# DeltaNet in a hybrid decoder layer: unnormalised queries, z in token order, first-level masks multiplied in beforehand, jobs in a new order

## The chip, the cores and the metric

The kernel runs on one core of one Trainium2 chip. The metric is the device time of one execution in microseconds (us); less is better. Five engines work side by side, each through its own instruction queue in program order: TensorE (PE, with its weight loads shown as PEld), VectorE (DVE), ScalarE (ACT), GpSimd (POOL) and SyncE (SP, which here starts the DMAs). They wait for one another by semaphores only.

## What is computed

One decoder layer over 256 tokens of width 2048: RMSNorm, one wide projection, two mixers side by side (a gated DeltaNet and a sliding-window attention), a gated merge, an output projection, and an MLP. All of it is in float32; each big matrix product is done as three fast ones, with the weights and the activations split into a high and a low part. The change touches the DeltaNet alone. Cut to what matters:

```python
qkv_c = silu(causal_depthwise_conv(qkv, conv_w))          # 4 taps along the tokens
q, k, v = split(qkv_c, 3)                                 # 16 heads of 128
q = q * rsqrt(sum(q * q) + 1e-6)                          # l2_normalize, per token and head
k = k * rsqrt(sum(k * k) + 1e-6)
beta = sigmoid(b_logit);  g = -exp(a_log) * softplus(a_logit + dt_bias)
q = q * 128 ** -0.5                                       # chunks of 64 tokens from here
gamma = exp(where(causal, decay_i - decay_j, -inf))       # decay = cumsum(g)
a_low = where(strict, (k * beta) @ k.T * gamma, 0)
sol   = solve(a_low + eye(64), [v * beta, k * beta * exp(decay)])
qk    = (q @ k.T) * gamma
# for each of the 4 chunks in turn, with the state S (128 x 128 per head):
v_new = u - w @ S
o     = (q * exp(decay)) @ S + qk @ v_new
S     = S * chunk_decay + k_dec.T @ v_new
o = rms_norm(o, norm_g) * silu(z)
```

## The kernel before

**Big products.** PE takes 512 output columns at a time (an *output*, `output`, lines 269 to 293). One output has 8 chunks of weights; each chunk is a DMA of 512 KB into `raw`, which ACT copies to `w_hi` (`split`, L653) and DVE turns into `w_lo` (L996). Chunk c+3 is split at the head of the work for chunk c on both engines. A chunk gives PE two *steps* of six matmuls each (L287 to L289).

**DeltaNet jobs.** Four windows of four outputs (k, q, v and z of four heads) feed `rawg`. While PE runs the 64 steps of one window, the DeltaNet of the four heads before (a *group*) is done in between: after step h of the big product every engine calls `gdn_step(h, g)`, which holds the job that belongs to this step. The steps stand in a table by hand (L66 to L74). Each of PE, ACT and DVE walks the same list in its own queue: for chunk c first `split(c + 3)`, then the jobs of step 2c, then those of step 2c+1; after the last chunk of an output it reads the accumulator (`read`, L875 and L1284). A job that must wait for another engine holds up all that stands behind it in its queue. GpSimd has a list of its own (`group`, L1415 to L1452). The group g = 3 runs in five straight outputs behind the loop.

**The steps of a group**, with their number in the table before:
- `FRONT` (k 0, q 1, v 25, z 37): PE turns the projected tile by 8 transposes (L316), ACT takes it with the fourth tap of the convolution (L726; for z it takes the tanh, L711).
- `TAPS`, `TANH`, `SILU`: DVE adds the other taps (L1051, three jobs each), ACT makes the tanh of half of it (L732), DVE makes the silu (L1057).
- `BACK` (k 10, q 16, v 34): PE turns it back (L345). For k and q ACT squares and sums 8 tiles (L738), DVE scales the sums (L1039), GpSimd raises them to the power -1/2 (`power`, L1418), and ACT multiplies (`NORM`, k 13, q 19, L744).
- `TK` 16 and `TQ` 21: PE turns the normalised k and q again (L354), ACT and DVE copy them to `kq` (L750, L755, L1076).
- `ROWS` 11: PE adds up the decays (L361, L362), DVE and ACT make the exponentials (L1068 to L1071, L759 to L761), GpSimd multiplies masks in (L1427 to L1434).
- `KKQ` 22: PE multiplies k by k and q by k (L376); DVE multiplies the results with the masked gammas (L1081 to L1083). GpSimd (L1437 to L1440) and DVE (L1087, L1089) make the matrices of the first level of the inverse from them.
- `INV` 25: five levels of a blockwise inverse, each with a first pass at step 25+3l and a second at 26+3l (L384); ACT copies in between (L765), DVE subtracts (L1093, L1096).
- `QTM` 40, then `P1`, `P2`, `P3`: the recurrence over four chunks (L423, L432, L440; ACT L775; DVE L1112, L1119, L1127).
- the end: the sum of squares of o (ACT L781), its power -1/2, o times it (DVE L1136), `OT` 63: PE turns o (L316), DVE multiplies with gain and silu(z) (L1145), ACT and DVE split it into `og_hi` and `og_lo`.

Of the kernel before, what the change touches and what calls it, by code (L numbers as in the profile page):

```python
# [1553 lines left out]
```

## Time and profile before

| | |
|---|---|
| median of 3 runs | 1945.68 us (1942.75 to 1945.89) |
| the profiled execution | 1942.99 us, of it 1941.2 us span |
| PE busy | 1885.3 us, 97% of the span |
| DVE / ACT / POOL busy | 1099.7 / 885.4 / 120.6 us |
| granted TensorE clock, mean | 0.989 |

The profile shows one execution. A line of the groups names the source line, the engine, the operation and its tile, then the count, the busy time and the mean of one, then how long the engine stood idle just before and what ended that. "PEclk" is the share of full speed that TensorE was granted. The four groups of the DeltaNet lie between about 121 and 740 us.

### The profile page before, as it was taken

The page shows a single profiled execution, that of the slowest core. Times are in us where ns is not written, and L with a number is a line of the kernel's source. Part 1 is how long each engine was busy: PE and PEld are TensorE (multiplying, and loading weights), DVE is VectorE, ACT ScalarE, POOL GpSimd, SP SyncE. Part 2 cuts the span into 40 slices and gives each one's busy share as a digit, 9 for nine tenths or more (in the row PEclk, how much of TensorE's full clock was granted, in tenths as well). Part 3 has the DMA queues.
Part 4 walks back from the last instruction along what each step waited for, and adds up shares of the span by engine and source line. Part 5 has one row for each costly group of instructions (what it writes and reads, how often), then busy time and mean ns, then how long its engine had stood idle before and what let it go on. Part 6 is the DMA issues. An engine that isn't in the chain of part 4 may idle for free.

```text
span 1941.2 us, 29129 instructions
## 1 busy us (share of the span) xinstructions
PE 1885.3 (97%) x10816; PEld 1554.7 (80%) x10816; DVE 1099.7 (57%) x1438; ACT 885.4 (46%) x1382; POOL 120.6 (6%) x86
## 2 busy tenths in 40 slices
PE   7998998998998999999999999999999999999997
PEld 6887877877877888888888888888888888888886
DVE  5366676676676665666555555555544455555544
ACT  5344345354354345555444445444433344444442
POOL 0005014014014000000000000000000000000000
PEclk9899999999999999999999999999999999999999
DMA  7353333333333354444456666555555555555553
GB/s 256 126 163 119 110 131 109 110 130 109 115 124 115 114 167 152 141 152 141 161 195 201 201 199 208 183 189 177 191 192 192 192 190 189 185 186 192 195 191 124
DMA packets 87953, 316.36 MB, mean 163 GB/s; under 512 B 9648, under 2 KB 10160, under 8 KB 87728
## 3 DMA queue, kind: packets, MB, share of 16 engines
q1 hardware_dynamic: 86992, 312.64, 48.9%
q0 software_dynamic: 576, 2.10, 0.4%
q8 instruction: 78, 1.28, 0.3%
q10 hardware_dynamic: 288, 0.18, 0.0%
q14 instruction: 19, 0.16, 0.0%
HBM read 312.79 MB, written 2.10 MB: 162 GB/s over the span
## 4 chain that ended last, share of the span: by engine, by line
PE 53%; issue 38%; DVE 3%; POOL 3%; ACT 1%; DMA 0%; DVEq 0%; ACTq 0%; POOLq 0%; SPq 0%
PE acc L287 15%; PE acc L289 14%; PE acc L288 14%; PE J L384 4%; PE J L432 1%; PE J L316 1%; POOL rg L1418 1%; PE J L423 1%; ACT w_hi L653 1%; PE J L440 1%; DVE cT L1051 1%; DVE qn L1051 1%; PE J L475 1%; PE J L304 0%; POOL mats L1440 0%
## 5 line engine op out<-in xcount | busy, mean ns | idle before, releaser
L996 DVE TENSOR_TENSOR w_lo<-raw,w_hi 128x1024 fp32r<-128x1024 f32 x584 | 725.3, 1244 | 638.0 <-ACT w_hi L653 636.6
L653 ACT ACTIVATE w_hi<-raw 128x1024 fp32r<-128x1024 f32 x584 | 618.7, 1061 | 681.7 <-PE acc L289 679.0
L287 PE MATMUL acc<-w_hi,hT_hi 128*128 128x512 f32 x1440 | 582.1, 404 | 8.9 <-issue 4.4
L289 PE MATMUL acc<-w_hi,hT_lo 128*128 128x512 f32 x1440 | 564.7, 392 | 0.0
L288 PE MATMUL acc<-w_lo,hT_hi 128*128 128x512 f32 x1440 | 564.5, 392 | 0.0
L287 PEld LDWEIGHTS acc<-w_hi,hT_hi 128*128 128x128 f32 x1440 | 272.4, 189 | 71.8 <-issue 8.4
L289 PEld LDWEIGHTS acc<-w_hi,hT_lo 128*128 128x128 f32 x1440 | 272.1, 189 | 58.7
L288 PEld LDWEIGHTS acc<-w_lo,hT_hi 128*128 128x128 f32 x1440 | 272.6, 189 | 52.5 <-issue 1.0
L287 PE MATMUL acc<-w_hi,act_hi 128*128 128x512 f32 x512 | 199.3, 389 | 0.0
L289 PE MATMUL acc<-w_hi,act_lo 128*128 128x512 f32 x512 | 199.2, 389 | 0.0
L288 PE MATMUL acc<-w_lo,act_hi 128*128 128x512 f32 x512 | 199.2, 389 | 0.0
L289 PEld LDWEIGHTS acc<-w_hi,act_lo 128*128 128x128 f32 x512 | 96.1, 188 | 20.1
L287 PEld LDWEIGHTS acc<-w_hi,act_hi 128*128 128x128 f32 x512 | 96.1, 188 | 19.9
L288 PEld LDWEIGHTS acc<-w_lo,act_hi 128*128 128x128 f32 x512 | 96.1, 188 | 19.7
L287 PE MATMUL acc<-w_hi,og_hi 128*128 128x512 f32 x256 | 102.2, 399 | 0.0
L289 PE MATMUL acc<-w_hi,og_lo 128*128 128x512 f32 x256 | 99.8, 390 | 0.0
L288 PE MATMUL acc<-w_lo,og_hi 128*128 128x512 f32 x256 | 99.8, 390 | 0.0
L384 PEld LDWEIGHTS J<-mats 64*64 64x64 f32 x2048 | 66.5, 140 | 24.9 <-issue 24.9
L384 PE MATMUL J<-mats 64*64 64x64 f32 x2048 | 72.6, 226 | 10.7 <-POOL mats L1440 10.7
L287 PEld LDWEIGHTS acc<-w_hi,og_hi 128*128 128x128 f32 x256 | 48.1, 188 | 11.9 <-issue 2.7
L289 PEld LDWEIGHTS acc<-w_hi,og_lo 128*128 128x128 f32 x256 | 48.1, 188 | 10.4
L288 PEld LDWEIGHTS acc<-w_lo,og_hi 128*128 128x128 f32 x256 | 48.1, 188 | 9.2
(210 smaller groups left out, 1522.4 us busy)
## 6 DMA issues: line engine op xcount, KB each, us to landing
raw<-weights SPq DMA_DIRECT2D x584, 512.0 KB, 3.3
xres<-x SPq DMA_DIRECT2D x4, 512.0 KB, 7.5
xres<-x POOLq DMA_DIRECT2D x4, 512.0 KB, 5.6
y<-nat SPq DMA_DIRECT2D x4, 512.0 KB, 2.7
fgain_sb<-fgain SPq DMA_DIRECT2D x1, 1024.0 KB, 5.2
masks_sb<-masks SPq DMA_DIRECT2D x1, 640.0 KB, 11.0
zs<-w_ba SPq DMA_DIRECT2D x1, 256.0 KB, 9.9
dist_sb<-dist SPq DMA_DIRECT2D x1, 192.0 KB, 3.4
```

The source lines that it names most:

```text
L287: mm(o, aT_hi[:, kt, tok], w_hi[:, c % RING, w], start=(c == 0 and k == 0), stop=False)
L288: mm(o, aT_hi[:, kt, tok], w_lo[:, c % RING, w], start=False, stop=False)
L289: last = mm(o, aT_lo[:, kt, tok], w_hi[:, c % RING, w], start=False, stop=(c == nch - 1 and k == CK - 1))
L316: ins = tr(J[:, b0 + m // 2, (m % 2) * T + t * P:(m % 2) * T + (t + 1) * P], src[:, t, m * P:(m + 1) * P], ident)
L384: ins = mm(J[r, bank, u * C:(u + 1) * C], lhs[r, u], rhs[r, u], start=True, stop=True)
L423: ins = mm(J[:, 0, hd * P:(hd + 1) * P], kq[:, hd, c * P:(c + 1) * P], S[:, hd], start=True, stop=True)
L432: ins = mm(J[:, 1, hd * P:(hd + 1) * P], solve[kr, t * HG + hd].rearrange("p a c -> p (a c)"), RH[kr, hd * P:(hd + 1) * P], start=True, st ...
L440: ins = mm(J[:, 2, hd * P:(hd + 1) * P], kn[kr, t, hd * P:(hd + 1) * P], VO[kr, hd * P:(hd + 1) * P], start=True, stop=True)
L475: ins = tr(J[:, 2 + pb, b * P:(b + 1) * P], prob[:, pb, b * P:(b + 1) * P], ident)
L653: A(w_hi[:, slot], raw[:, slot], ACT.Copy).then_inc(hi_ready, 1)
L996: tt(w_lo[:, slot], raw[:, slot], w_hi[:, slot].bitcast(F32), ALU.subtract).then_inc(lo_ready, 1)
L1051: ins = stt(out=dst[:, m, s:T], in0=J[:, b, o:o + T - s], scalar=cwg[:, n, m, 3 - s:4 - s], in1=dst[:, m, s:T], op0=ALU.mult, op1=ALU.add)
```

## The change

It does four things.
- **Queries.** q is no longer normalised ahead of the products. Its silu is written straight into `kq` in token order on the free axis; BACK q only serves the sum of squares, `NORM` q, `TQ` and the copies behind it are gone. Since rms_norm follows, the length of q enters as a larger epsilon (`rg[:, 3]`, `nq_done`) in the scale of o.
- **z.** It stays in token order: no turn at `FRONT`, one tanh of 1024 columns and one product (`Z_TANH` 34 and 35). The halves of 64 tokens are swapped when the accumulator is read (`halves`), so that each reading of z is two instructions instead of one. The product of o with its scale now takes silu(z) with it: eight instructions on DVE in place of one. Behind `OT`, ACT makes `og_hi` from PSUM by four instructions, and DVE `og_lo` by four.
- **Masks.** GpSimd multiplies `nlow1` and `nup1` into the gammas ahead of `KKQ`; behind it DVE has four products and two additions of the identity, GpSimd only the masks of the levels.
- **Order.** A new table: `ROWS` at 2, `FRONT` q at 7, `BACK` k at 9, `NORM_K` 11, `TK` 14, `KKQ` 17, `BACK` q 19, `INV` 22, `QTM` 37, `OT` 62.

```diff
-FRONT = {ITEM_K: 0, ITEM_Q: 1, ITEM_V: 25, ITEM_Z: 37}
-BANK = {ITEM_K: 0, ITEM_Q: 2, ITEM_V: 2, ITEM_Z: 2}
-TAPS = {ITEM_K: (0, 1, 2), ITEM_Q: (3, 5, 7), ITEM_V: (26, 28, 31)}
-TANH = {ITEM_K: 3, ITEM_Q: 9, ITEM_V: 32}
-SILU = {ITEM_K: 4, ITEM_Q: 10, ITEM_V: 33}
-BACK = {ITEM_K: 10, ITEM_Q: 16, ITEM_V: 34}
-NORM = {ITEM_K: 13, ITEM_Q: 19}
-ROWS, TK, TQ, KKQ, INV, QTM, OT = 11, 16, 21, 22, 25, 40, 63
-P1, P2, P3 = (40, 45, 50, 55), (42, 47, 52, 57), (44, 49, 54, None)
+FRONT = {ITEM_K: 0, ITEM_Q: 7, ITEM_V: 25}
+BANK = {ITEM_K: 0, ITEM_Q: 2, ITEM_V: 2}
+TAPS = {ITEM_K: (0, 1, 3), ITEM_Q: (9, 11, 12), ITEM_V: (26, 28, 30)}
+TANH = {ITEM_K: 4, ITEM_Q: 13, ITEM_V: 31}
+SILU = {ITEM_K: 5, ITEM_Q: 15, ITEM_V: 32}
+BACK = {ITEM_K: 9, ITEM_Q: 19, ITEM_V: 34}
+ROWS, ROWS_EXP, NORM_K, TK, KKQ, INV, Z_TANH, QTM, OT = 2, 3, 11, 14, 17, 22, 34, 37, 62
+P1, P2, P3 = (37, 42, 47, 52), (39, 44, 49, 55), (41, 46, 51, None)
+O_SQ, O_SUM, O_SCALE = (48, 56), 57, 60
 
 PAIRS = HQ // 2
...
                 if h == KKQ:
 
-                    pe.wait_ge(kq_a, 2 * g + 2)
+                    pe.wait_ge(kq_a, g + 1)
                     pe.wait_ge(kq_d, g + 1)
 
+                    pe.wait_ge(silu_done, 4 * g + 2)
                     pe.sem_inc(step_begun, 1)
...
+                for n in (ITEM_K, ITEM_Q, ITEM_V):
+                    if h == BACK[n]:
+                        pe.wait_ge(silu_done, 4 * g + (n + 1))
+                        if n == ITEM_Q:
+
+                            pe.wait_ge(xu_link, g + 1)
+                        for t in range(NT):
+                            for m in range(HG):
+                                src = kq_q(m, t) if n == ITEM_Q else cT[:, m, t * P:(t + 1) * P]
+                                ins = tr(J[:, BANK[n] + t, m * P:(m + 1) * P], src, ident)
+                        ins.then_inc(back_T, 1)
+                if h == TK:
+
+                    pe.wait_ge(norm_done, g + 1)
+                    for t in range(NT):
+                        for m in range(HG):
+                            ins = tr(J[:, t, m * P:(m + 1) * P], kn[:, t, m * P:(m + 1) * P], ident)
+                    ins.then_inc(qk_T, 1)
 
...
-                    if h == NORM[n]:
-                        act.wait_ge(nr_done, 2 * g + (n + 1))
-                        for u in range(U):
-                            ins = A(dst3[:, u], J[:, BANK[n] + u // HG, (u % HG) * P:(u % HG + 1) * P], ACT.Copy,
-                                    scale=rg[:, n, u:u + 1])
-                        ins.then_inc(norm_done, 1)
+                if h == NORM_K:
+                    act.wait_ge(nr_done, g + 1)
+                    for u in range(U):
+                        ins = A(kn3[:, u], J[:, u // HG, (u % HG) * P:(u % HG + 1) * P], ACT.Copy, scale=rg[:, 0, u:u + 1])
+                    ins.then_inc(norm_done, 1)
                 if h == TK:
-                    act.wait_ge(qk_T, 2 * g + 1)
+                    act.wait_ge(qk_T, g + 1)
                     dst = kq[:, :, 0:T].rearrange("p h (a c) -> p h a c", a=4)[:, :, 0:4:3]
                     A(dst, J[:, 0].rearrange("p (h a c) -> p h a c", h=HG, a=2), ACT.Copy).then_inc(kq_a, 1)
-                if h == TQ:
-
-                    act.wait_ge(qk_T, 2 * g + 2)
-                    for t in range(NT):
-                        ins = A(kq[:, :, t * T + C:t * T + C + P], J[:, 2 + t].rearrange("p (h t) -> p h t", h=HG), ACT.Copy)
-                    ins.then_inc(kq_a, 1)
-                if h == ROWS:
+                if h == Z_TANH:
+
+                    act.wait_ge(silu_done, 4 * g + 3)
+                    act.wait_ge(rawg_a, 4 * g + 4)
+                    act.wait_ge(rawg_d, 4 * g + 4)
+                    A(zs2, z_raw, ACT.Tanh, scale=0.5).then_inc(tanh_done, 1)
+                if h == ROWS_EXP:
                     act.wait_ge(arg_done, g + 1)
                     A(mat(M_X), mat(M_X), ACT.Exp)
...
                 if h == OT:
+                    act.wait_ge(o_T, g + 1)
                     for b in range(2):
-                        act.wait_ge(og_f, 2 * g + (3 + b))
-                        A(og_hi[:, bass.ds(g * HG + 2 * b, 2), :], cT[:, 2 * b:2 * b + 2], ACT.Copy).then_inc(og_hi_done, 1)
+                        src = J[:, b].rearrange("p (u a c) -> p u a c", u=4, a=2)
+                        dst = og_hi[:, bass.ds(g * HG + 2 * b, 2), :].rearrange("p h (t a c) -> p (h t) a c", t=NT, a=2)
+                        for a in range(2):
+                            ins = A(dst[:, :, a], src[:, :, 1 - a], ACT.Copy, scale=gdn_gain)
+                        ins.then_inc(og_hi_done, 1)
 
...
+                        if n == ITEM_Z:
+                            for r, to in halves():
+                                ins = A(rawg[to, n, 0], acc[r, n % 2, 0], ACT.Copy, scale=row_scale(0, 0)[r])
+                            ins.then_inc(rawg_a, 1)
+                        else:
+                            A(rawg[:, n, 0], acc[:, n % 2, 0], ACT.Copy, scale=row_scale(0, 0)).then_inc(rawg_a, 1)
...
+                if h == BACK[ITEM_Q] + 1:
+                    dve.wait_ge(nsq_done, 2 * g + 2)
+
+
+                    f = 4 * EPS * P
+                    for r, to in halves():
+                        ins = ts(rg[to, 3], rg[r, 1], f, 4 * EPS * f, ALU.mult, ALU.add)
+                    ins.then_inc(nq_done, 1)
...
-                        dst, th = (qnT, vbT) if n == ITEM_Q else (cT[:], zs[:])
-                        stt(out=dst, in0=th, scalar=1.0, in1=dst, op0=ALU.add, op1=ALU.mult).then_inc(silu_done, 1)
+                        if n == ITEM_Q:
+                            dst = kq[:].rearrange("p h (t e) -> p h t e", t=NT)[:, :, :, C:C + P]
+                            src, th = (a.rearrange("p h (t e) -> p h t e", t=NT) for a in (qnT, vbT))
+                        else:
+                            dst, src, th = cT[:], cT[:], zs[:]
+                        stt(out=dst, in0=th, scalar=1.0, in1=src, op0=ALU.add, op1=ALU.mult).then_inc(silu_done, 1)
...
                     dve.wait_ge(kkq_done, g + 1)
-                    dve.wait_ge(mask_done, 5 * g + 5)
+                    dve.wait_ge(mask_done, 6 * g + 6)
                     kk, kqp = (J[:, b].rearrange("p (u c) -> p u c", u=U) for b in (2, 3))
-                    tt(mat(M_V), kk, mat(M_V), ALU.mult)
-                    tt(mat(M_AT), kk, mat(M_B1), ALU.mult)
-                    tt(mat(M_KQ), kqp, mat(M_KQ), ALU.mult).then_inc(at_ready, 1)
+                    tt(mat(M_AT), kk, mat(M_B1), ALU.mult).then_inc(at_ready, 1)
+                    tt(mat(M_X), kk, mat(M_V), ALU.mult)
+                    tt(mat(M_U), kk, mat(M_U), ALU.mult)
+                    tt(mat(M_KQ), kqp, mat(M_KQ), ALU.mult).then_inc(xu_link, 1)
                 if h == KKQ + 1:
 
-                    dve.wait_ge(at_ready, g + 1)
-                    tt(mat(M_U), mat(M_AT), over(nup1, U), ALU.mult).then_inc(u0_ready, 1)
-                    dve.wait_ge(u0_ready, 2 * g + 1)
+                    dve.wait_ge(xu_link, g + 1)
+                    tt(mat(M_X), mat(M_X), over(eye64, U), ALU.add)
                     tt(mat(M_U), mat(M_U), over(eye64, U), ALU.add).then_inc(u0_ready, 1)
                 for lv in range(LEVELS):
                     if h == INV + 3 * lv + 1:
...
+                    dve.wait_ge(nq_done, g + 1)
+                    stt(out=rg[:, 2], in0=rg[:, 2], scalar=4.0 / P, in1=rg[:, 3], op0=ALU.mult, op1=ALU.add).then_inc(ossq_done, 1)
+                if h == O_SCALE:
                     dve.wait_ge(or_done, g + 1)
-                    tt(qn3, qn3, wide(rg[:, 2], P), ALU.mult).then_inc(on_done, 1)
+                    dve.wait_ge(silu_done, 4 * g + 4)
+                    for u in range(U):
+                        ins = stt(out=qn3[:, u], in0=qn3[:, u], scalar=rg[:, 2, u:u + 1], in1=zs3[:, u], op0=ALU.mult, op1=ALU.mult)
+                    ins.then_inc(on_done, 1)
                 if h == OT:
...
-                power(0, nssq_done, 2 * g + 1, nr_done)
 
                 pool.wait_ge(exp_done, g + 1)
                 tt(mat(M_KQ), mat(M_X), over(upi, U), ALU.mult).then_inc(mask_done, 1)
                 tt(mat(M_B1), mat(M_X), mat(M_B0), ALU.mult).then_inc(mask_done, 1)
-                pool.wait_ge(mask_done, 5 * g + 2)
+                power(0, nssq_done, g + 1, nr_done)
+                pool.wait_ge(mask_done, 6 * g + 2)
                 tt(mat(M_B1), mat(M_B1), over(up, U), ALU.mult).then_inc(mask_done, 1)
-                tt(mat(M_V), mat(M_U), over(low, U), ALU.mult).then_inc(mask_done, 1)
-                power(1, nssq_done, 2 * g + 2, nr_done)
-                pool.wait_ge(mask_done, 5 * g + 4)
+                tt(mat(M_V), mat(M_U), over(nlow1, U), ALU.mult).then_inc(mask_done, 1)
+                pool.wait_ge(mask_done, 6 * g + 4)
                 tt(mat(M_V), mat(M_V), wide(scu(BETA), C), ALU.mult).then_inc(mask_done, 1)
+                tt(mat(M_U), mat(M_B1), over(nup1, U), ALU.mult).then_inc(mask_done, 1)
 
                 pool.wait_ge(at_ready, g + 1)
-                tt(mat(M_X), mat(M_V), over(nlow1, U), ALU.mult).then_inc(xu_link, 1)
                 tt(mat(M_B0), mat(M_AT), over(up_level[0], U), ALU.mult).then_inc(bt_ready, 1)
-                pool.wait_ge(xu_link, g + 1)
-                tt(mat(M_X), mat(M_X), over(eye64, U), ALU.add).then_inc(x0_ready, 1)
                 for lv in range(1, LEVELS):
                     if lv >= 2:
 
@@ -1445,7 +1457,7 @@
                     tt(mat(M_B0 + lv % 2), mat(M_AT), over(up_level[lv], U), ALU.mult).then_inc(bt_ready, 1)
                     if lv == 1:
 
-                        pool.wait_ge(qk_T, 2 * g + 1)
+                        pool.wait_ge(qk_T, g + 1)
                         tt(kn3, kn3, wide(scu(K_DEC), P), ALU.mult).then_inc(kdec_done, 1)
```

## Rows read from the trace of the kernel before

**Rows 1.** The page: two of its costliest groups, busy us and mean ns.

```profile
L996 DVE TENSOR_TENSOR w_lo<-raw,w_hi 128x1024 fp32r<-128x1024 f32 x584 | 725.3, 1244 | 638.0 <-ACT w_hi L653 636.6
L653 ACT ACTIVATE w_hi<-raw 128x1024 fp32r<-128x1024 f32 x584 | 618.7, 1061 | 681.7 <-PE acc L289 679.0
```

**Rows 2.** Waits of PE: who waited for whom, us in total, times, longest.

```profile
PE J L354 <- ACT qn L744: 10.9, 4, 3.0
PE J L384 <- POOL mats L1440: 10.7, 4, 2.7
...
PE J L354 <- ACT kn L744: 3.5, 4, 0.9
PE J L361 <- DVE qn L1051: 3.1, 3, 1.6
```

**Rows 3.** Timeline of PE, group 1: start us, us, engine, line, what.

```profile
266.06 1.03 PE L316 MATMUL J<-masks_sb,rawg 128*128 128x128 f32 x8
...
268.31 1.03 PE L316 MATMUL J<-masks_sb,rawg 128*128 128x128 f32 x8
...
297.64 0.39 PE L287 MATMUL acc<-w_hi,hT_hi 128*128 128x512 f32 x1
...
299.00 0.39 PE L287 MATMUL acc<-w_hi,hT_hi 128*128 128x512 f32 x1
```

**Rows 4.** Timeline of PE at the inverse, groups 1 and 2 (the latter from 462).

```profile
318.66 1.97 PE L384 MATMUL J<-mats 64*64 64x64 f32 x32 [2.68 <-POOL mats L1440]
...
324.71 0.50 PE L287 MATMUL acc<-w_hi,hT_hi 128*128 128x512 f32 x1
...
327.66 1.15 PE L384 MATMUL J<-mats 64*64 64x64 f32 x32
...
332.35 0.50 PE L287 MATMUL acc<-w_hi,hT_hi 128*128 128x512 f32 x1
...
462.18 1.97 PE L384 MATMUL J<-mats 64*64 64x64 f32 x32 [2.69 <-POOL mats L1440]
...
469.67 0.49 PE L287 MATMUL acc<-w_hi,hT_hi 128*128 128x512 f32 x1
```

**Rows 5.** Busy us by stretches: PE, PEld, DVE, ACT, POOL, then PEclk, DMA share.

```profile
320.00:323.00 3.00, 3.00 (x28) 2.25 (x27) 0.75 (x1) 1.54 (x2) 2.89 (x2) 0.70 0.10 37
```

**Rows 6.** Timeline of ACT, group 1.

```profile
284.72 1.06 ACT L732 ACTIVATE vb<-qn 128x1024 f32<-128x1024 f32 x1 [4.78 <-DVE qn L1051]
...
286.63 0.26 ACT L738 ACTIVATE kn<-J 128x128 f32<-128x128 f32 x1
...
288.54 0.25 ACT L738 ACTIVATION_READ_ACCUMULATOR kn<-J 128x1 f32 x1
...
293.11 2.16 ACT L744 ACTIVATE kn<-J,rg 128x128 f32<-128x128 f32 x8
```

**Rows 7.** Timeline of DVE, group 1.

```profile
283.05 1.64 DVE L1051 SCALAR_TENSOR_TENSOR qn<-J,cwg,qn 128x253 f32<-128x253 f32 x4
...
287.90 1.22 DVE L1057 SCALAR_TENSOR_TENSOR qn<-vb,qn 128x1024 f32<-128x1024 f32 x1
289.03 0.17 DVE L1039 TENSOR_SCALAR rg<-rg 128x8 f32<-128x8 f32 x1
...
296.25 2.05 DVE L996 TENSOR_TENSOR w_lo<-raw,w_hi 128x1024 fp32r<-128x1024 f32 x1 [1.54 <-ACT w_hi L653]
...
300.45 0.68 DVE L1076 COPY kq<-J 128x512 f32<-128x512 f32 x1
...
390.78 1.13 DVE L1127 SCALAR_TENSOR_TENSOR S<-S,scg,J 128x128 f32<-128x128 f32 x4
```

**Rows 8.** Timeline of POOL, group 1.

```profile
269.35 1.04 POOL L1423 TENSOR_TENSOR mats<-scg,masks_sb 128x512 f32<-128x512 f32 x1
289.28 1.64 POOL L1418 TENSOR_TENSOR rg<-rg,stat 128x8 f32<-128x8 f32 x1 [18.88 <-DVE rg L1039]
...
301.29 2.71 POOL L1418 TENSOR_TENSOR rg<-rg,stat 128x8 f32<-128x8 f32 x1 [1.84 <-DVE rg L1039]
```

More of the change, by code:

```diff
@@ L169, in hybrid_trunk, with kq_q, halves @@
         qnT, vbT = (a[:].rearrange("p t n -> p (t n)").rearrange("p (h t) -> p h t", h=HG) for a in (qn, vb))
+        zs2 = zs[:].rearrange("p h t -> p (h t)")
+        zs3 = zs2.rearrange("p (u e) -> p u e", u=U)
+        z_raw = rawg[:, ITEM_Z].rearrange("p t n -> p (t n)")
+        def kq_q(m, t):
+            return kq[:, m, t * T + C:t * T + C + P]
+        def halves():
+            return [(slice(ck * C, ck * C + C), slice((1 - ck) * C, (2 - ck) * C)) for ck in range(2)]
         qn3, kn3, vb3 = (a[:].rearrange("p t (h e) -> p (t h) e", h=HG) for a in (qn, kn, vb))
@@ L705, in gdn_step @@
             def gdn_step(h, g):
-                if h == FRONT[ITEM_Z]:
-                    act.wait_ge(front_T, 4 * g + 4)
-                    act.wait_ge(silu_done, 4 * g + 3)
-                    for b in range(2):
-                        ins = A(zs[:, 2 * b:2 * b + 2].rearrange("p a t -> p (a t)"), J[:, 2 + b], ACT.Tanh, scale=0.5)
-                    ins.then_inc(tanh_done, 1)
                 for n in (ITEM_K, ITEM_Q, ITEM_V):
                     if h == FRONT[n]:
-                        act.wait_ge(front_T, 4 * g + (n + 1))
+                        act.wait_ge(front_T, 3 * g + (n + 1))
                         if n == ITEM_K:
                             act.wait_ge(par_ready, g + 1)
-                        else:
-                            if n == ITEM_V:
-                                act.wait_ge(back_T, 3 * g + 2)
+                        if n == ITEM_V:
+                            act.wait_ge(back_T, 3 * g + 2)
                         dst = qnT if n == ITEM_Q else cT
@@ L914, in gate @@
                 return ops
-            act.wait_ge(og_lo_done, 2 * NG)
+            act.wait_ge(og_lo_done, 2 * NG + 2)
             def mix1(j):
@@ L1026, in gdn_step @@
                     V.tensor_copy(cwg[:], conv_w[:, :, bass.ds(g * HG, HG), :]).then_inc(par_ready, 1)
-                if h == FRONT[ITEM_Z] + 1:
+                if h == Z_TANH + 1:
                     dve.wait_ge(tanh_done, 4 * g + 4)
-                    for b in range(2):
-                        zb = zs[:, 2 * b:2 * b + 2].rearrange("p a t -> p (a t)")
-                        ins = stt(out=zb, in0=zb, scalar=1.0, in1=J[:, 2 + b], op0=ALU.add, op1=ALU.mult)
-                    ins.then_inc(silu_done, 1)
-                for i, n, dst in ((0, ITEM_K, kn3), (1, ITEM_Q, qn3)):
-                    if h == BACK[n] + 1:
-                        dve.wait_ge(nsq_done, 2 * g + (i + 1))
-                        f = (1.0, float(P))[i]
-                        ts(rg[:, i], rg[:, i], f, 4 * EPS * f, ALU.mult, ALU.add).then_inc(nssq_done, 1)
+                    stt(out=zs2, in0=zs2, scalar=1.0, in1=z_raw, op0=ALU.add, op1=ALU.mult).then_inc(silu_done, 1)
+                if h == BACK[ITEM_K] + 1:
+                    dve.wait_ge(nsq_done, 2 * g + 1)
+                    ts(rg[:, 0], rg[:, 0], 1.0, 4 * EPS, ALU.mult, ALU.add).then_inc(nssq_done, 1)
+                if h == BACK[ITEM_Q] + 1:
[4 more added lines that the diff above has]
+                    ins.then_inc(nq_done, 1)
                 for n in (ITEM_K, ITEM_Q, ITEM_V):
```

93 lines of the change are left out of this document (36 added, 57 removed).

## The prediction

> **What bounds the kernel now.** I read the page first. TensorE is busy over nearly the whole span, so the time is the sum of what PE issues plus the little it waits. The two groups that take most of DVE and ACT are the splits of the weights, one each per chunk, 1.24 and 1.06 us in the mean [rows 1]; the reader should keep them in mind, because each stands in the same queue as the DeltaNet's jobs. Second I read the waits of PE, which are few and all inside the DeltaNet: before the turn of the normalised q 10.9 us, before the first level of the inverse 10.7 us, before the turn of the normalised k 3.5 us, before ROWS 3.1 us [rows 2]. Together 28.2 us in four groups, 7.05 us a group. Third, the timeline of PE, for what a step costs. Six matmuls of the big product, an ordinary step, take 299.00 - 297.64 = 1.36 us; a step with a turn of eight transposes takes 268.31 - 266.06 = 2.25 us, so a turn costs 0.89 us [rows 3]. Fourth, the timeline at the inverse. After the wait at its first level the two passes and the step between take 324.71 - 318.66 = 6.05 us, and at the next level, undisturbed, 332.35 - 327.66 = 4.69 us [rows 4]. The difference of 1.36 us is the clock: PE was granted 0.70 of full speed in that stretch, thus partly the level of 1.2 GHz instead of 2.4 [rows 5], after two waits within some 16 us. In group 2 the same passes take 469.67 - 462.18 = 7.49 us, a loss of 2.80 [rows 4]. These are the least and the largest of four; I take 1.8 us a group, since three of the four lie near the low end.
>
> So a group now loses 7.05 us to waits and about 1.8 to the clock, 8.85 us.
>
> **The change, part by part.**
>
> *Two turns less.* The turn of z at FRONT and the one at TQ go. Each is 0.89 us of PE time with nothing beside it, for PE is the bound: 1.78 us a group, 7.1 in all.
>
> *The wait at TQ* goes with its job: 10.9 / 4 = 2.7 us a group. *The wait at ROWS* goes too, if GpSimd's tables are there at step 2. Today they end at 269.35 + 1.04 = 270.39 [rows 8], 4.3 us after the window's first turn started at 266.06 [rows 3]. They wait for DVE, which is then still at work on the group before; OT comes a step earlier, 1.36 us, so about 2.9. PE gets to ROWS a turn and two steps after that start, 0.89 + 2.72 = 3.6. The margin is 0.7 us; without the earlier OT the wait would be 0.7.
>
> *The wait at the first level* goes. Today GpSimd makes three products in a row between KKQ and INV, and that is the wait of 2.7 us. After the change GpSimd has one, and DVE makes X and U: four products of the 0.68 us kind (128x512, one operand in PSUM) [rows 7], then a split and two additions. PE has five steps and one turn between KKQ and INV, some 7.8 us; DVE needs 2.8 for the products, up to 2.05 for a split beside GpSimd [rows 7] and at most 1.7 for each addition, about 7.6 with the latencies. It just fits. 2.7 us gone, and if PE has not waited before, 1.8 of the clock with it.
>
> *What becomes late instead.* This is the heart of my forecast. The new table puts only five steps between BACK k (9) and TK (14), with no other PE job in them, and KKQ at 17. I follow the chain from the end of BACK k's transposes on (time 0), with every queue in its order.
> - ACT: squares of k, 288.79 - 286.63 = 2.16 us [rows 6]; then it splits a chunk, about 1.0 once the overlap with the neighbour is taken off its 1.06. 3.15.
> - DVE can't scale the sums before it has split the same chunk (1.24) [rows 1], then 0.17 [rows 7]. 4.5.
> - GpSimd: the power -1/2, 1.64 us [rows 8]. 6.25, with 0.1 for latencies.
> - ACT: NORM_K, 2.16 us [rows 6]. 8.45. TK can start.
> - PE is there after five steps, 5 x 1.36, at 6.65. It waits **1.8 us**, takes the turn (0.89) and three more steps (4.1) and stands at KKQ at 13.45.
> - KKQ also waits for the silu of q (`silu_done`), and that hangs on the same ACT queue: behind NORM_K stands a split (1.0), then DVE's split of that chunk, 1.24 or, beside GpSimd's masks, 2.05 [rows 7]; I take 1.6, between them, as the masks end within it. Then the last tap of q, 1.64 [rows 7]. ACT: the tanh, 1.06 [rows 6], and a split, 1.0. DVE: its split, 1.2, the copy to kq, 0.6, the silu, 1.22 [rows 7]. Sum 8.45 + 1.0 + 1.6 + 1.6 + 1.06 + 1.0 + 1.2 + 0.6 + 1.2 = 17.7.
> - So PE waits another 17.7 - 13.45 = **4.3 us** at KKQ. Both together 6.1 us a group. The whole of this replaces 0.9 + 2.7 + 0.8 us that PE waits ahead of KKQ today.
>
> The power's row is not sure. The one that I take, 1.64 us, ran beside a DVE product with an operand in PSUM; another ran beside DVE's split and took 2.71 [rows 8]. In the new order DVE has a tap of the convolution with an operand in PSUM at that time, so I take 1.64 and keep 1.07 us a group, 4.3 in all, for the range. The Trainium skill (GPSIMD Engine Reference, section 1, Specifications) says that GpSimd shares its SBUF interface with VectorE and meets contention from DVE instructions with two SBUF inputs or in a two-port mode. By that rule the price is the lower one as well; the two rows agree with it.
>
> *The tail.* The scale of o stands at step 60 for OT at 62. DVE's job starts when ACT and DVE have split the chunk of that step, 1.06 + 1.24 and latencies, about 2.4 us after the end of step 59. It is now eight instructions of 128x128; four such take 1.13 [rows 7], eight 2.2. That makes 4.6 or 4.7, and PE is there after three steps, 4.08. A wait of **0.6 us** a group. Below nothing it can't go; above, 1.2, if each instruction costs twice the part that I read from the four.
>
> *The rest.* Four instructions of ACT from PSUM at OT instead of two, DVE's eight products for o, the two halves of z: all beside PE, and the next window's first turn comes over 3 us after OT. Inside the inverse I find one place where ACT's tanh of v stands ahead of the copy for level 3 and comes 0.15 us late; others pass with 0.2 to 0.3 us to spare. 0.15 a group, up to 0.6 when the spare fails. The first BACK q waits for DVE's products, level with PE. No DMA is moved; SP's queue gets nothing new, and the splits run two chunks ahead of PE through all the waits above.
>
> *The clock.* A wait of 4.3 us behind one of 1.8 is longer than any that the trace shows, so I expect PE to fall to 1.2 GHz at KKQ in each group. I price it as the drops of today, 1.8 us; bounds 0 and 2.8 [rows 4].
>
> **The sum.** Today a group loses 7.05 + 1.8 = 8.85, and the clock in group 3 falls once more, about 1.5 in all: 4 x 8.85 + 1.5 = 36.9; with the turns, 7.1, there are 44.0 us to be had. The new group loses 6.1 + 0.6 + 0.15 + 1.8 = 8.65, in four 34.6. The gain is 9.4 us. The profiled execution took 1942.99 us, 1.79 more than its span; it lies 2.7 below the median of the runs. So 1933.6 against that execution, and against the median 1945.68 - 9.4 = **1936.3 us**.
>
> **The rivals.**
> - *The waits really vanish* (the order works as a schedule without stalls). Then only the tail and the inverse cost, 4 x 0.75 = 3: 44.0 - 3 = 41 gained, 1904.7. For it speaks that all four waits of today lose their cause; against it, the chain above, in which every link is a row and the queues are strict. Chance 0.08.
> - *The waits stay but the clock holds.* Gain 9.4 + 7.2, 1929.1. For it speaks that the wait at TQ of 3.0 us, alone, was followed by steps at full speed in group 1. Chance 0.12.
> - *The chain grows and the waits only move.* If the chain from BACK k to the silu of q is 1.4 to 3.3 us longer than I make it, the result is within 0.2% of before; 2.35 us more gives 1945.7. Chance 0.13.
> - *Slower.* GpSimd and DVE get in each other's way in that chain: the power takes 2.71 instead of 1.64, and DVE's two later splits 2.05 instead of 1.6 and 1.2, together 2.4 us a group; with the clock loss at 2.8 instead of 1.8 a group costs 3.4 more than I say, 13.6 in all, which ends at 1949.9. It decides from 2.35 us a group on. Against it: GpSimd's four masks end about when the first of the two splits does. Chance 0.08.
>
> **How the numbers follow.** The forecast itself has 0.59, its own range 1930 to 1942. About 0.2%, 3.9 us, is what a measurement of this kernel can tell from no change. Faster: 0.08 + 0.12 + nearly all of 0.59 = 0.76; same: 0.13 and a little of the forecast, 0.16; slower 0.08. The range leaves out the first rival and most of the last: 1925 to 1945.
>
> **What would show it.** The waits of PE should list TK on ACT's kn with about 1.8 us, four times, and KKQ on DVE's silu of q (L1057 before) with about 4.3, four times, and nothing before the inverse. The page should have 64 transposes less. PE's clock should dip at KKQ and not at the first level. OT should wait 0.6 us for DVE's product of o. I am wrong if PE reaches KKQ without a wait (then ACT's and DVE's queues run ahead of the steps more than I think), or if waits appear in the levels of the inverse, where my margins are thinnest.

## The result, and the profile after

The changed kernel takes **1933.86 us** (median of four runs, 1933.71 to 1933.97), the kernel before beside it 1945.79 (1942.75 to 1948.06). The ratio is 0.994, with a 95% interval of 0.9922 to 0.9957: 0.4 to 0.8% faster. The forecast was 1936.3, range 1925 to 1945.

The page after, its head and its clock:

```profile
span 1932.1 us, 28995 instructions
## 1 busy us (share of the span) xinstructions
PE 1878.6 (97%) x10752; PEld 1549.1 (80%) x10752; DVE 1102.7 (57%) x1466; ACT 877.4 (45%) x1350; POOL 104.2 (5%) x78
...
PEclk9899999999999999999999999999999999999999
```

PE has 64 instructions less, as two turns of eight in four groups must give. The waits of PE in the whole execution (who waited for whom, us in total, times, longest), the answer to [rows 2]:

```profile
PE J L364 <- DVE kq L1067: 15.8, 4, 4.0
PE J L383 <- ACT kn L740: 6.7, 4, 1.7
...
PE J L348 <- POOL mats L1438: 2.4, 2, 1.2
PE J L326 <- DVE qn L1149: 1.8, 4, 0.5
PE acc L297 <- ACT rawg L876: 1.8, 1, 1.8
PE acc L297 <- issue: 1.7, 1, 1.7
```

Three waits of before are gone: that of TQ on ACT, that of the first level of the inverse on GpSimd, and that of ROWS on DVE; ROWS now waits for GpSimd's tables in two of four groups. The first line is new: KKQ (L364) waits for the silu of q (L1067), four times, 4.0 us at the longest. The second is TK, 1.7 where it was 0.9. OT (L326) waits 0.5 us in each group for DVE's eight products of o. The last two lines are the gaps of PE at the start of the two looped windows.

The timeline of PE in group 1 shows the two, and the clock behind the second:

```profile
293.58 1.09 PE L383 MATMUL J<-masks_sb,kn 128*128 128x128 f32 x8 [1.67 <-ACT kn L740]
...
302.70 2.96 PE L364 MATMUL J<-kq 128*64 128x64 f32 x64 [3.92 <-DVE kq L1067]
...
309.11 1.03 PE L376 MATMUL J<-masks_sb,kq 128*128 128x128 f32 x8
...
314.17 1.15 PE L390 MATMUL J<-mats 64*64 64x64 f32 x32
```

From KKQ to the turn of q behind it 309.11 - 302.70 = 6.41 us pass; without the drop it is 4.87 (below). The granted clock of that stretch (columns as in [rows 5]):

```profile
302.00:307.00 5.00, 4.30 (x67) 3.97 (x68) 3.55 (x5) 0.52 (x1) 0.43 (x1) 0.66 0.57 199
```

The first level of the inverse starts at 314.17 without a wait and takes 1.15 us instead of 1.97 [rows 4].

**Where the time went.** The two profiled executions differ by 9.1 us of span, and not all of it is the DeltaNet's. From the first turn of group 0 to the first turn of probabilities in the attention the kernel before takes 734.7 - 122.71 = 612.0 us, the changed one 725.6 - 125.49 = 600.1; from there to the end both take 1206.5 (1941.2 - 734.7, 1932.1 - 725.6). So the DeltaNet gained 11.9 us, and the changed one's execution reached it 2.8 us later, in a part that the change does not touch. The rows, before and after (one row each of PE's timeline and of the line of the turns, with the first and last start):

```profile
122.71 1.03 PE L316 MATMUL J<-masks_sb,rawg 128*128 128x128 f32 x8
...
L475 PE MATMUL J<-masks_sb,prob x96: 270/273/280, 734.7 to 941.1; 128*128 128x128 f32 x96
```

```profile
125.49 1.03 PE L326 MATMUL J<-masks_sb,rawg 128*128 128x128 f32 x8
...
L479 PE MATMUL J<-masks_sb,prob x96: 270/273/280, 725.6 to 932.0; 128*128 128x128 f32 x96
```

Below I call this stretch the DeltaNet's. It repeats to about a microsecond where the whole time doesn't, and its sum closes: PE's waits in it, the gaps at the window starts among them, fell from 33.5 to 30.4 (3.1), the clock cost 8.7 before and 7.2 after (1.5; a drop is counted as the time of its steps less the time of the same steps at full clock), the turns give 7.1; together 11.7 of the 11.9.

### The profile page after: what moved, and what is told of

It reads as the page before. It is cut to its first block, busy times and chain, and to the rows that moved or that the text cites. A ratio compares the mean times of both kernels' runs of the same rounds, so it can differ in the third digit from the quotient of the medians.

```text
span 1932.1 us, 28995 instructions
## 1 busy us (share of the span) xinstructions
PE 1878.6 (97%) x10752; PEld 1549.1 (80%) x10752; DVE 1102.7 (57%) x1466; ACT 877.4 (45%) x1350; POOL 104.2 (5%) x78
## 4 chain that ended last, share of the span: by engine, by line
PE 54%; issue 39%; DVE 3%; ACT 2%; POOL 1%; DMA 0%; DVEq 0%; ACTq 0%; POOLq 0%; SPq 0%
PE acc L297 15%; PE acc L298 14%; PE acc L299 14%; PE J L390 3%; PE J L436 1%; ACT w_hi L657 1%; PE J L326 1%; PE J L427 1%; PE J L364 1%; PE J L444 1%; DVE cT L1057 1%; PE J L479 1%; DVE w_lo L1000 1%; PE J L314 0%; POOL mats L1442 0%
## 5 line engine op out<-in xcount | busy, mean ns | idle before, releaser
L657 ACT ACTIVATE w_hi<-raw 128x1024 fp32r<-128x1024 f32 x584 | 618.3, 1061 | 654.6 <-PE acc L299 652.3
L297 PEld LDWEIGHTS acc<-w_hi,og_hi 128*128 128x128 f32 x256 | 48.1, 188 | 11.9 <-issue 2.7
```

The costliest lines, as they stand in the source:

```text
L297: mm(o, aT_hi[:, kt, tok], w_hi[:, c % RING, w], start=(c == 0 and k == 0), stop=False)
L657: A(w_hi[:, slot], raw[:, slot], ACT.Copy).then_inc(hi_ready, 1)
```

## The experiments

Each kernel is the changed one with the edit shown. The time is the median; "stretch" is the DeltaNet's from the profile.

### The changed kernel again

> The changed kernel once more, as the measure for the others on this chip: 1933 to 1936 us, with the waits of its first profile (KKQ 3.95 and TK 1.7 us a group).

1934.94 us (1930.45 to 1935.8), stretch 727.6 - 126.38 = 601.2. Its waits are those of the first profile: 15.8 at KKQ, 6.7 at TK. Two executions of one program thus differ by 1.1 us in the stretch, and this is the yardstick. At KKQ the clock cost 1.5 us in each of the four groups here, 6.2 in all instead of 7.2.

### NORM_K one step later

```diff
-ROWS, ROWS_EXP, NORM_K, TK, KKQ, INV, Z_TANH, QTM, OT = 2, 3, 11, 14, 17, 22, 34, 37, 62
+ROWS, ROWS_EXP, NORM_K, TK, KKQ, INV, Z_TANH, QTM, OT = 2, 3, 12, 14, 17, 22, 34, 37, 62
```

> The changed kernel with one number moved: NORM_K at step 12 instead of 11, so that in ACT's queue the split of the next chunk stands ahead of the eight products of k, not behind them. Theory A (the wait at KKQ is a queue effect: DVE's last tap of q waits for a split that stands behind NORM_K's wait for GpSimd): the wait of PE at KKQ falls from 3.95 us a group to about 0.5, the half-clock stretch behind it (1.57 us a group) goes, the wait at TK stays at 1.7; together 4 x 5.0 = 20 us, 1914 us against 1933.9. Rival B (the chain is long whatever the order within ACT, since ACT and DVE have that much to do there): KKQ still waits 3 to 4 us, 1932 to 1935 us.

1917.08 us (1913.83 to 1917.55), ratio to before 0.9855 (0.9814 to 0.9896); a second time 1916.49 (below). Stretch 582.2. One number in the table gives more than the whole change did. ACT's timeline of the changed kernel, where the split (L657) stands behind the eight products of k (L740):

```profile
291.35 2.18 ACT L740 ACTIVATE kn<-J,rg 128x128 f32<-128x128 f32 x8 [3.09 <-POOL rg L1433]
293.36 1.11 ACT L657 ACTIVATE w_hi<-raw 128x1024 fp32r<-128x1024 f32 x1
```

And DVE's, which idles 3.35 us for that split and only then comes to the last tap (L1057):

```profile
289.51 1.65 DVE L1057 SCALAR_TENSOR_TENSOR qn<-J,cwg,qn 128x254 f32<-128x254 f32 x4
294.50 1.47 DVE L1000 TENSOR_TENSOR w_lo<-raw,w_hi 128x1024 fp32r<-128x1024 f32 x1 [3.35 <-ACT w_hi L657]
295.90 1.63 DVE L1057 SCALAR_TENSOR_TENSOR qn<-J,cwg,qn 128x253 f32<-128x253 f32 x4
```

With NORM_K at 12, DVE goes from one to the next without a gap:

```profile
285.37 1.65 DVE L1057 SCALAR_TENSOR_TENSOR qn<-J,cwg,qn 128x254 f32<-128x254 f32 x4
286.93 1.21 DVE L1000 TENSOR_TENSOR w_lo<-raw,w_hi 128x1024 fp32r<-128x1024 f32 x1
288.06 1.64 DVE L1057 SCALAR_TENSOR_TENSOR qn<-J,cwg,qn 128x253 f32<-128x253 f32 x4
```

and PE's waits, and the KKQ of group 1 with the turn of q behind it, are

```profile
PE J L383 <- ACT kn L740: 6.7, 4, 1.7
...
PE J L364 <- DVE kq L1067: 4.8, 4, 1.3
```

```profile
295.85 2.08 PE L364 MATMUL J<-kq 128*64 128x64 f32 x64 [1.18 <-DVE kq L1067]
...
300.72 1.04 PE L376 MATMUL J<-masks_sb,kq 128*128 128x128 f32 x8
```

Theory A holds: 11.0 us of wait gone, and 300.72 - 295.85 = 4.87 us at full clock. Wait and clock give (15.8 - 4.8) + 7.2 = 18.2; the stretch shortened by 17.9 and the median by 16.8, less than the 20 expected, since 1.2 us a group stay where I had 0.5: DVE's next split ran beside GpSimd's last mask and took 2.19 us.

### The masks of the first level behind KKQ again

```diff
-                    tt(mat(M_AT), kk, mat(M_B1), ALU.mult).then_inc(at_ready, 1)
-                    tt(mat(M_X), kk, mat(M_V), ALU.mult)
-                    tt(mat(M_U), kk, mat(M_U), ALU.mult)
-                    tt(mat(M_KQ), kqp, mat(M_KQ), ALU.mult).then_inc(xu_link, 1)
+                    tt(mat(M_V), kk, mat(M_V), ALU.mult)
+                    tt(mat(M_AT), kk, mat(M_B1), ALU.mult)
+                    tt(mat(M_KQ), kqp, mat(M_KQ), ALU.mult).then_inc(at_ready, 1)
...
                 pool.wait_ge(at_ready, g + 1)
+                tt(mat(M_X), mat(M_V), over(nlow1, U), ALU.mult).then_inc(xu_link, 1)
                 tt(mat(M_B0), mat(M_AT), over(up_level[0], U), ALU.mult).then_inc(bt_ready, 1)
+                pool.wait_ge(xu_link, g + 1)
+                tt(mat(M_X), mat(M_X), over(eye64, U), ALU.add).then_inc(x0_ready, 1)
```

(The waits that go with it are left out: PE's first pass waits for `x0_ready` again.)

> The changed kernel with the masks of the first inversion level multiplied in behind KKQ again, as before: three products of GpSimd between KKQ and the first level (X, the mask of level 0, X plus identity), the order untouched. Theory A (the new distance of five steps and a turn between KKQ and INV, 7.8 us, covers 2.1 + 5.8 us of that chain nearly by itself): a wait of 0.2 to 0.6 us a group at the first level, the clock untouched, 1935 to 1936.5 us. Rival B (the masks are what took the wait away): 2.7 us a group and 1.8 of the clock come back, about 1952 us.

1933.5 us (1930.2 to 1934.41), stretch 722.7 - 123.19 = 599.5: no difference from the changed kernel. Not even the small wait of theory A is there. Rival B falls. GpSimd's three products and PE's first pass behind them:

```profile
304.64 2.20 POOL L1453 TENSOR_TENSOR mats<-mats,masks_sb 128x512 f32<-128x512 f32 x1 [13.23 <-DVE mats L1095]
306.79 1.75 POOL L1454 TENSOR_TENSOR mats<-mats,masks_sb 128x512 f32<-128x512 f32 x1
308.51 1.74 POOL L1456 TENSOR_TENSOR mats<-mats,masks_sb 128x512 f32<-128x512 f32 x1
```

```profile
310.39 1.15 PE L390 MATMUL J<-mats 64*64 64x64 f32 x32
```

The last of them ends at 310.25 and the pass starts at 310.39, on its own time. Five steps and a turn between KKQ and the inverse, where there were three steps and a turn, hide the whole chain of GpSimd. The wait of 10.7 us [rows 2] was taken away by the order; the masks add nothing to that here.

PE ran at half clock behind KKQ in this run too, and that gave GpSimd more time. With NORM_K at 12 the clock held, and there the rows are (KKQ starts at 295.85)

```profile
298.06 0.69 DVE L1091 TENSOR_TENSOR mats<-J,mats 128x512 f32<-128x512 f32 x1 [0.57 <-PE J L364]
...
304.69 0.68 DVE L1099 TENSOR_TENSOR mats<-mats,masks_sb 128x512 f32<-128x512 f32 x1
```

```profile
305.82 1.15 PE L390 MATMUL J<-mats 64*64 64x64 f32 x32
```

DVE starts its products 2.21 us after KKQ has started, and PE reaches the inverse 9.97 us after that start. With the masks back GpSimd's last product ended 310.25 - 302.68 = 7.57 us after DVE's first had started. So at full clock I estimate 2.21 + 7.57 = 9.78 us: it would still fit, by 0.2 us. No run here shows it.

### One turn more

```diff
                     pe.wait_ge(vb_done, g + 1)
 
+                    turn_group(rawg[:, ITEM_Z], 2, z_turned)
                     pe.sem_inc(step_begun, 1)
```

(The new semaphore `z_turned` is left out.)

> The changed kernel plus one turn of z (8 transposes into a free bank, result unused) just ahead of QTM. Theory A (PE is the bound, a turn costs what PE issues, 0.89 us, in each of four groups): +3.6 us, 1937.4 us. Rival B (a turn falls into waits of PE or is absorbed by one that is due later): no change, 1934 us.

1938.29 us (1935.15 to 1940.02). Against the changed kernel that is 4.4 us more than its first median and 3.4 more than its second; the stretch, 731.1 - 126.45 = 604.7, is 4.5 and 3.4 us longer. All waits are as before the edit. Theory A, 3.6 us, lies in between. The whole time can't tell it more closely, since the clock behind KKQ cost 8.2 us here and 7.2 and 6.2 in those two. The timeline can: in group 1 the way from the last level's second pass to QTM takes 354.25 - 349.29 = 4.96 us in the changed kernel and 357.07 - 351.23 = 5.84 with the turn in it, 0.88 more. A turn costs what PE issues.

### The early steps as before, the later ones as in the change

```diff
-FRONT = {ITEM_K: 0, ITEM_Q: 7, ITEM_V: 25}
+FRONT = {ITEM_K: 0, ITEM_Q: 1, ITEM_V: 28}
-TAPS = {ITEM_K: (0, 1, 3), ITEM_Q: (9, 11, 12), ITEM_V: (26, 28, 30)}
+TAPS = {ITEM_K: (0, 1, 2), ITEM_Q: (3, 5, 7), ITEM_V: (29, 31, 33)}
...
-BACK = {ITEM_K: 9, ITEM_Q: 19, ITEM_V: 34}
-ROWS, ROWS_EXP, NORM_K, TK, KKQ, INV, Z_TANH, QTM, OT = 2, 3, 11, 14, 17, 22, 34, 37, 62
-P1, P2, P3 = (37, 42, 47, 52), (39, 44, 49, 55), (41, 46, 51, None)
-O_SQ, O_SUM, O_SCALE = (48, 56), 57, 60
+BACK = {ITEM_K: 10, ITEM_Q: 22, ITEM_V: 37}
+ROWS, ROWS_EXP, NORM_K, TK, KKQ, INV, Z_TANH, QTM, OT = 11, 11, 13, 16, 20, 25, 37, 40, 63
+P1, P2, P3 = (40, 45, 50, 55), (42, 47, 52, 57), (44, 49, 54, None)
+O_SQ, O_SUM, O_SCALE = (48, 58), 59, 61
```

(Left out: PE's wait for the exponentials moves from `FRONT` q to KKQ, and ROWS also waits for the taps of q.)

> The new arithmetic (queries, z, masks) with the first part of the table as before (FRONT q 1, BACK k 10, ROWS 11, NORM_K 13, TK 16) and the rest three steps later than in the changed kernel (KKQ 20, BACK q 22, INV 25, QTM 40, P steps and OT 63 as before). Theory A (the gain lies in the work and waits taken away, and the new order gives part of it back at KKQ, TK and OT): no wait at KKQ, 0.9 us a group at TK and 0.8 at ROWS as before, none at OT, no half-clock stretch: 1933.9 - 15.8 - 3.2 + 0.7 - 1.8 - 6.3 = 1907.5 us. Rival B (the waits only move with the steps, since the chain from k to the silu of q is as long as ever): 1930 to 1936 us.

1942.2 us (1940.29 to 1944.8), stretch 608.7. Both theories miss: KKQ doesn't wait, as A says, but TK does, and far longer than either has it. PE's waits and GpSimd's timeline:

```profile
PE J L385 <- ACT kn L742: 24.5, 4, 6.2
```

```profile
294.97 1.29 POOL L1443 TENSOR_TENSOR mats<-mats,masks_sb 128x512 f32<-128x512 f32 x1 [21.93 <-ACT mats L758]
296.22 2.24 POOL L1444 TENSOR_TENSOR mats<-mats 128x512 f32<-128x512 f32 x1
298.43 1.63 POOL L1435 TENSOR_TENSOR rg<-rg,stat 128x8 f32<-128x8 f32 x1
```

The power of k (L1435) starts when two masks are done, and those wait for the exponentials. The change had moved the power behind them in GpSimd's own list; with ROWS at 2 this costs nothing, with ROWS at 11 it holds up TK. I had moved a step back past three queues and overlooked the fourth.

### The same with GpSimd's power in front

The edit is shown against the kernel of the last section.

```diff
+                power(0, nssq_done, g + 1, nr_done)
+
                 pool.wait_ge(exp_done, g + 1)
                 tt(mat(M_KQ), mat(M_X), over(upi, U), ALU.mult).then_inc(mask_done, 1)
                 tt(mat(M_B1), mat(M_X), mat(M_B0), ALU.mult).then_inc(mask_done, 1)
-                power(0, nssq_done, g + 1, nr_done)
```

> The kernel with the early steps as before (1942 us), with one more thing put back: in GpSimd's list the power -1/2 of k stands ahead of the two masks, as it did before the change, not behind them. Theory A (the list of GpSimd is the fourth queue of the new order: with ROWS at 11 the power waits for the exponentials and then for 1.3 and 2.2 us of masks): the wait at TK falls from 6.1 to 0.9 us a group (20.9 us in all), the half-clock stretch behind it, 2.3 us a group, goes; 1942 - 20.9 - 9.2 = 1912 us. Rival B (the late wait has another cause, such as ACT's exponentials or the split ahead of NORM_K): TK still waits over 3 us, above 1925 us.

1919.07 us (1916.24 to 1919.78), stretch 584.5. Theory A in kind: 23 us come from one instruction's place. It is 7 us above the 1912 forecast, and the waits say where most of that is:

```profile
PE J L385 <- ACT kn L742: 7.0, 4, 1.8
...
PE J L378 <- DVE mats L1096: 1.7, 4, 0.5
```

TK keeps 3.4 us more than the 3.6 that I had left it, and the turn of BACK q (L378) now waits 1.7 for DVE's products. The waits at ROWS (4.5) and QTM (2.7) don't count here: they stood at 4.6 and 2.7 already in the run before. The other 2 us are not traced. TK waits 1.8 us, not 0.9, because before the change the turn of BACK q, 0.89 us [rows 3], stood between ROWS and TK and covered half of it. So the new arithmetic with the early steps as before is 14.8 us faster than with the new order: 1919.1 against 1933.9. This kernel gains about 27 us on the one before, and the new table gave more than half of that back. The 27 us are not the arithmetic's alone: this table too keeps five steps between KKQ and the inverse, and the section on the masks showed that the wait there hangs on them.

### Two steps later

```diff
-FRONT = {ITEM_K: 0, ITEM_Q: 7, ITEM_V: 25}
+FRONT = {ITEM_K: 0, ITEM_Q: 7, ITEM_V: 27}
...
-ROWS, ROWS_EXP, NORM_K, TK, KKQ, INV, Z_TANH, QTM, OT = 2, 3, 11, 14, 17, 22, 34, 37, 62
-P1, P2, P3 = (37, 42, 47, 52), (39, 44, 49, 55), (41, 46, 51, None)
-O_SQ, O_SUM, O_SCALE = (48, 56), 57, 60
+ROWS, ROWS_EXP, NORM_K, TK, KKQ, INV, Z_TANH, QTM, OT = 3, 4, 12, 16, 19, 24, 36, 39, 63
+P1, P2, P3 = (39, 44, 49, 54), (41, 46, 51, 56), (43, 48, 53, None)
+O_SQ, O_SUM, O_SCALE = (50, 57), 58, 61
```

(BACK q and v, and the taps, tanh and silu of v move by two as well.)

> The changed order with NORM_K at 12 and, beyond that, everything from TK on two steps later (TK 16, KKQ 19, INV 24, QTM 39), the last P2 at 56, the scale of o at 61, OT at 63, ROWS at 3. Theory A (what is left of waits is distance only, 1.7 us at TK and 1.2 at KKQ against 2.7 us for two steps; OT's 0.45 goes with one more step for DVE's eight products): against the kernel with NORM_K at 12 alone, 1917.1 us, it saves 6.7 + 4.8 + 1.8 + 2.4 = 15.7 less 0.2 us a group that remain: 1902 us. Rival B (the waits move into the tail: OT at 63 makes the next window's first steps late, the recurrence squeezed by one step waits at P2): 1908 to 1917 us.

1926.43 us (1925.82 to 1931.06), 9 us slower than NORM_K at 12 alone; the stretch is 717.6 - 123.10 = 594.5, 12 longer. A falls. B holds in so far as waits only move, but the largest of them isn't in the tail, and the sum is worse than I put it:

```profile
PE J L364 <- DVE kq L1086: 9.9, 4, 2.6
PE acc L297 <- issue: 5.6, 2, 2.9
...
PE J L390 <- ACT mats L760: 3.2, 4, 0.8
PE J L326 <- ACT mats L756: 2.7, 3, 1.2
```

TK no longer waits, but KKQ now waits for the copy of k (L1086), which has moved to the other side of an output's end, where the accumulator is read; an ACT job stands ahead of a copy inside the inverse; q's turn waits for the exponentials; and the longest gap at the start of a window grew from 1.8 to 2.9 us, with half the clock behind that one. Several things were changed at once, so the share of each is not shown.

### One step later

```diff
-FRONT = {ITEM_K: 0, ITEM_Q: 7, ITEM_V: 25}
+FRONT = {ITEM_K: 0, ITEM_Q: 7, ITEM_V: 26}
...
-ROWS, ROWS_EXP, NORM_K, TK, KKQ, INV, Z_TANH, QTM, OT = 2, 3, 11, 14, 17, 22, 34, 37, 62
-P1, P2, P3 = (37, 42, 47, 52), (39, 44, 49, 55), (41, 46, 51, None)
-O_SQ, O_SUM, O_SCALE = (48, 56), 57, 60
+ROWS, ROWS_EXP, NORM_K, TK, KKQ, INV, Z_TANH, QTM, OT = 2, 3, 12, 15, 18, 23, 35, 38, 62
+P1, P2, P3 = (38, 43, 48, 53), (40, 45, 50, 55), (42, 47, 52, None)
+O_SQ, O_SUM, O_SCALE = (51, 56), 57, 59
```

(BACK q 20 and v 35; of v the taps 27, 29, 31, tanh and silu 33.)

> The changed order with NORM_K at 12, everything from TK to the recurrence one step later (TK 15, KKQ 18, BACK q 20, INV 23, QTM 38), the last P2 where it was (55), v's tanh and silu both at 33, and the scale of o at 59 instead of 60, ahead of a split; OT stays at 62. Theory A (what is left is distance, as long as the last step of the window isn't used for OT and no ACT job stands ahead of a copy in the inverse): against NORM_K at 12 alone, 1917.1 us, 1.36 us a group less at TK and KKQ together and 0.45 at OT: 4 x 1.8 = 7.2, 1910 us. Rival B (a later KKQ only meets a later wait, as when it was two steps later): 1915 to 1922 us.

> NORM_K at 12 alone, once more beside the kernel above: 1917 us, within 2 us.

1913.36 us (1909.92 to 1915.82), ratio to before 0.9823 (0.9803 to 0.9844), the fastest kernel here; NORM_K at 12 alone took 1916.49 (1913.34 to 1916.86) beside it. The ranges of the two overlap, but the stretches, 578.7 and 582.3, are further apart than the 1.1 us of the yardstick. Half of the 7.2 us that I expected came:

```profile
PE J L364 <- DVE kq L1086: 5.5, 4, 1.5
...
PE J L390 <- DVE solve L1110: 2.7, 4, 0.7
...
PE J L383 <- ACT kn L740: 1.3, 4, 0.3
```

TK fell from 6.7 to 1.3, and OT's 1.8 are gone, since DVE multiplies o in an idle place ahead of a split; but KKQ rose from 4.9 to 5.5, and a new wait of 0.7 us a group stands at QTM.

## Why the prediction was right

**The sum.** The gain forecast was 9.4 us; 11.9 were measured, both as the difference of the medians and as the stretch of the DeltaNet. The terms of the first profile:

| term, us a group | forecast | measured |
|---|---|---|
| wait at TK | 1.8 | 1.7 |
| wait at KKQ | 4.3 | 3.95 |
| clock behind KKQ | 1.8 | 1.8 (2.6 in group 0, 1.5 in the others) |
| wait at OT | 0.6 | 0.45 |
| wait at ROWS | 0 | 0.6 (1.2 in two groups) |
| wait in the inverse | 0.15 | 0 |
| first level, wait and clock | 0 | 0 |

The waits in the table came to 26.7 us instead of 27.4, 0.7 in favour of the change. Another 1.6 lie in waits that the sum left out, PE's gaps at the window starts and two short ones: 5.3 us before, 3.7 after. That the table comes so close is in part luck. ROWS cost 2.4 us that I had at nothing, and four terms that I had too high (TK, KKQ, OT, the inverse) gave back 3.1. And the clock behind KKQ, 1.8 us a group to the digit, was 1.5 in the repeated run and 2.1 in the one with a turn more, by the same waits.

**The heart of it held.** The chain from BACK k to the silu of q was followed queue by queue, and moving NORM_K behind a split showed that it is this order, not the amount of work, that makes KKQ wait. The power took 1.64 us, the row that I chose. Even the higher price that I kept for the range is not sure: in group 3 of the kernel before the same power lay beside a split of DVE too (590.08 to 591.31) and took 1.64. The forecast of 4.3 at KKQ is 0.35 too long from both ends. From the first square of k (285.13) the silu of q is there for PE after 17.57 us, where I had 17.7, since DVE's split beside GpSimd took 1.47 and not 1.6; and PE is there after 298.78 - 285.13 = 13.65, where I had 13.45, since the turn of k and three steps took 5.2 us and not 5.0. At TK the sum has a slip: 5 x 1.36 is 6.80 and not 6.65, which leaves a wait of 1.65 us. PE waited 1.67.

**What was off.** The margin of 0.7 us at ROWS did not hold: PE waited 1.2 us in groups 0 and 3, and in groups 1 and 2 the tables came only 0.1 and 0.2 us before it. I had taken 1.36 us for the earlier OT off the old time and nothing for the two halves of z, for which ACT and DVE each take two instructions where one stood, ahead of DVE's copy of the parameters; I had called them free, since they lie beside PE. Group 0, where no OT stands ahead, shows what they cost. Before and after:

```profile
121.55 0.75 DVE L1284 TENSOR_SCALAR rawg<-acc,stat 128x512 f32<-128x512 f32 x1 [0.34 <-PE acc L289]
```

```profile
125.75 1.05 POOL L1423 TENSOR_TENSOR mats<-scg,masks_sb 128x512 f32<-128x512 f32 x1
```

```profile
124.32 1.52 DVE L1296 TENSOR_SCALAR rawg<-acc,stat 64x512 f32<-64x512 f32 x2 [0.34 <-PE acc L299]
```

```profile
129.35 1.04 POOL L1438 TENSOR_TENSOR mats<-scg,masks_sb 128x512 f32<-128x512 f32 x1
```

DVE's reading of z takes 1.52 us instead of 0.75, and GpSimd's tables end 6.07 us after its start instead of 5.25, 0.8 later. The rest comes from reading group 1 for all four. Group 0 has no OT ahead that could come earlier. Groups 1 and 2 have PE's own gap of 1.7 and 1.8 us ahead of their first turn, which hides as much lateness; groups 0 and 3 have none.

The other way, PE's gaps at the start of the two looped windows fell from 4.4 to 3.5 us together, which I had not in the sum. They go with the step of OT: the four profiles here with OT at 63 have 4.4 to 5.6 us there, the seven with OT at 62 have 2.8 to 3.7. No run moved OT alone, so that OT is the cause is not shown.

The parts for the first level don't add up as written: 2.8, 2.05 and twice 1.7 make 8.25 us with bounds, not 7.6, and PE has 7.8. DVE took less, 313.10 - 305.80 = 7.3 us from its first product to the end of the second addition, and that fits even at full clock: with NORM_K at 12 the addition ended 305.82 - 305.37 = 0.45 us before PE came.

**Right for a reason that was put wrongly.** I gave the loss of the wait at the first level to the change as a whole, and told it as GpSimd having one product instead of three. With the three back the wait stays away. It was the distance in steps. Nor would the masks have done at the old distance, by an estimate from the rows with NORM_K at 12: DVE's second addition ends 305.37 - 295.85 = 9.5 us after KKQ's start, and with two steps less PE would stand there after 9.97 - 2.72 = 7.25.

**The rivals.** That all waits vanish did not come, nor that the clock holds: the level fell to 1.2 GHz at KKQ in every group (0.66 of full speed in the mean of that stretch). That GpSimd and DVE slow each other in the chain came in small: a split of 1.47 us here and of 2.19 with NORM_K at 12, but not the power.

## What to carry to other kernels

Where several engines walk one table of steps, a job's place is its place in each queue: look at what stands behind a job that waits, above all shared work like the splits here, and put the waiting job behind it. Moving one ACT job by one step was worth 17 us, more than the arithmetic and the order of the change together. A new order must be costed by its distances between dependent jobs on the bound engine, and every queue must be walked, that of the least busy engine too.

## What the runs showed of the hardware

GpSimd and VectorE slow each other markedly. In the changed kernel a DVE silu that takes 1.21 us when GpSimd is idle (that of q, at 301.34) took 2.31 beside GpSimd's product (that of k), and that took 2.27 where its neighbour took 1.30:

```profile
281.21 2.31 DVE L1067 SCALAR_TENSOR_TENSOR cT<-zs,cT 128x1024 f32<-128x1024 f32 x1
```

```profile
278.91 1.30 POOL L1441 TENSOR_TENSOR mats<-mats,masks_sb 128x512 f32<-128x512 f32 x1 [7.19 <-ACT mats L756]
280.17 2.27 POOL L1442 TENSOR_TENSOR mats<-mats 128x512 f32<-128x512 f32 x1
```

The Trainium skill (SBUF — State Buffer, section "Who interferes with whom") has it that only the port pair that the two share contends, and as an exclusive lock. The trace agrees in so far as the silu lost 1.10 us and the product 0.97, each about what the other had to do meanwhile; the taps, which read PSUM, took 1.63 to 1.65 us beside GpSimd as elsewhere.

The start of the program varies by several microseconds: the first turn of group 0 came between 122.71 and 126.82 us in the eleven profiles here, though nothing before it differs in what PE has to do, and at 125.49 and 126.38 in two of one kernel. The 20 us from 40 on had a granted clock of 0.72 in one and 0.66 in another, which are these two executions, before and the repeated changed kernel:

```profile
40.00:60.00 20.00, 20.00 (x115) 19.22 (x114) 5.18 (x9) 4.24 (x9) 0.00 (x0) 0.72 0.29 91
```

```profile
40.00:60.00 20.00, 20.00 (x107) 19.34 (x105) 4.82 (x5) 4.03 (x5) 0.00 (x0) 0.66 0.29 97
```

That is why the stretch is the better measure for a few microseconds.
